# First block's attention in batches of three branches per pair of heads and tile of queries, with the local branch's rows scaled on POOL

## The reference, cut to what matters

```python
s = jnp.einsum('bgnqd,bgkd->bgnqk', qb, k_cmp) * scale - slopes * d_c
p_cmp = masked_softmax(s, d_c >= 0)
o_cmp = jnp.einsum('bgnqk,bgkd->bgnqd', p_cmp, v_cmp)
...   # o_slc and o_win in the same way, from two other sets of keys and values
return g[..., 0:1] * o_cmp + g[..., 1:2] * o_slc + g[..., 2:3] * o_win
...
return o * jax.nn.silu(z)      # z = h @ its columns of w_in
```

## Time and profile before

| | us |
|---|---|
| median of 3 runs | 3018.0 |
| the profiled execution | 3018.1 |
| its span, first to last instruction | 3016.3 |
| attention stage, PE's first scores to its last product | 194.0 to 422.5 |

### The profile page before, as it was taken

How to read it: one execution, slowest core, us unless ns; L and a number is a source line. 1 busy time by engine, 2 the same in 40 slices (tenths; PEclk the granted TensorE clock), 3 DMA queues, 4 the chain that set the end, 5 groups by cost and what they waited for, 6 DMA issues and landing times. The chain is left out here.

```text
span 3016.3 us, 40331 instructions
## 1 busy us (share of the span) xinstructions
PE 2877.6 (95%) x16205; PEld 2346.1 (78%) x16205; DVE 1359.6 (45%) x2458; ACT 1139.6 (38%) x2067; POOL 1237.9 (41%) x593
## 2 busy tenths in 40 slices
PE   6999989999999979999998999999998999999998
PEld 4875558888988867677887999988787757888887
DVE  5436650342133233683542555532477642566620
ACT  4347762222244333343553422222343355422221
POOL 5432224454344432222222545554445422545553
PEclk9999999999999988999997999999999999999999
DMA  7310012222322211113222422233222223422222
GB/s 263 140 57 15 15 32 94 98 98 98 112 91 98 97 43 55 42 43 100 75 75 90 150 84 95 90 103 105 87 92 80 86 74 103 160 91 97 98 99 91
DMA packets 83457, 272.70 MB, mean 90 GB/s; under 512 B 9863, under 2 KB 10119, under 8 KB 83144
## 3 DMA queue, kind: packets, MB, share of 16 engines
q1 hardware_dynamic: 81936, 269.23, 26.8%
q10 hardware_dynamic: 1336, 0.89, 0.1%
HBM read 255.34 MB, written 14.75 MB: 90 GB/s over the span
## 5 line engine op out<-in xcount | busy, mean ns | idle before, releaser
L132 POOL TENSOR_TENSOR weights_lo<-weights_raw,weights_hi 128x1024 fp32r<-128x1024 f32 x415 | 1008.3, 2432 | 1356.6 <-ACT weights_hi L124 1356.4
L124 ACT ACTIVATE weights_hi<-weights_raw 128x1024 fp32r<-128x1024 f32 x415 | 437.6, 1058 | 1049.7 <-PE acc L491 540.8
L489 PE MATMUL acc<-h_hi,weights_hi 128*128 128x512 f32 (+2 forms) x1808 | 667.1, 369 | 28.3 <-ACT gate_tiles L2554 7.9
L490 PE MATMUL acc<-h_lo,weights_hi 128*128 128x512 f32 (+2 forms) x1808 | 640.1, 354 | 0.0
L491 PE MATMUL acc<-h_hi,weights_lo 128*128 128x512 f32 (+2 forms) x1808 | 639.7, 354 | 0.0
L489 PEld LDWEIGHTS acc<-h_hi,weights_hi 128*128 128x128 f32 x1808 | 346.4, 192 | 108.7 <-issue 53.0
L491 PEld LDWEIGHTS acc<-h_hi,weights_lo 128*128 128x128 f32 x1808 | 346.7, 192 | 45.9
L490 PEld LDWEIGHTS acc<-h_lo,weights_hi 128*128 128x128 f32 x1808 | 347.4, 192 | 41.5 <-issue 0.2
L535 PE MATMUL acc<-weights_hi,h_hi 128*128 128x256 f32 (+1 forms) x480 | 145.3, 303 | 8.0 <-DVE h_lo L997 5.2
L489 PE MATMUL acc<-y_hi,weights_hi 128*128 128x512 f32 (+2 forms) x392 | 141.6, 361 | 10.1 <-DVE full L2744 5.2
L825 ACT ACTIVATE probs<-probs,low 128x31 f32<-128x31 f32 (+5 forms) x276 | 138.4, 503 | 19.8 <-DVE low L792 19.2
(11 more groups left out here) (435 smaller groups left out, 5247.4 us busy)
## 6 DMA issues: line engine op xcount, KB each, us to landing
weights_raw<-in_stream SPq DMA_DIRECT2D x415, 512.0 KB, 3.4
weight_ring<-in_w_ada SPq DMA_DIRECT2D x24, 512.5 KB, 7.5
gates<-gate_tiles SPq DMA_DIRECT2D x24, 258.0 KB, 4.2
gate<-gates SPq DMA_DIRECT2D x8, 774.0 KB, 5.7
held<-gates SPq DMA_DIRECT2D x8, 768.0 KB, 6.0
gates<-gate_tiles SPq DMA_DIRECT2D x23, 256.0 KB, 4.1
flipped<-bias_rows SPq DMA_DIRECT2D x8, 320.0 KB, 4.3
x<-in_x SPq DMA_DIRECT2D x2, 1024.0 KB, 13.6
```

Source lines behind the costliest of these rows:

```text
L124: act.activation(self.hi[:, at % CUT, :], self.raw[:, at % RAW, :], ACT.Copy).then_inc(self.hi_done, 1)
L132: pool.tensor_tensor(self.lo[:, at % CUT, :], self.raw[:, at % RAW, :], self.hi[:, at % CUT, :].bitcast(F32), ALU.subtract).then_inc(self. ...
L489: pe.matmul(out, left[0], right[0], start=start, stop=False)
L490: pe.matmul(out, left[0], right[1], start=False, stop=False)
```

## The change

`BatchAttend` replaces `PairAttend` in this stage alone (the second and third blocks keep it). A batch is all three kinds for one pair and one tile: 32 batches.

- Step s on PE: weigh(s-3) for all kinds, scores(s) for all kinds, then the turns of batch s-2, four parts (selected and window for each head) in units of at most 512 columns: 1 unit for tile 0, 2 for tile 1, 4 for tiles 2 and 3. There is one `turn` bank and one set of four score banks. A slot is one unit, so a step has 1, 2 or 4 slots, 92 in all.
- On ACT a step is copy out, then for each unit a read and up to two (of 4 units), three (of 2) or six (of 1) exponentials of batch s.
- On DVE a step is six minima of batch s, one reciprocal for all six sums of batch s-1, the scaling of the selected and compressed rows (four), and a copy of the turned compressed rows of batch s-2 from PSUM (`cmp_t`), which PE's next weigh waits for.
- The window's rows (the local branch) are scaled on POOL, behind its tables.
- The compressed kind of both heads is one matmul (block-diagonal `k_blk`, `v_blk`, cleared by POOL in the stage before, filled by two copies each) and one turn of 128x128.
- `Dense` has one `acc` bank here, taken at the unit's last slot. The lead is 8 slots instead of 16, here and in `gated_output`.

```diff
+class BatchAttend(Lane):
+    SETS, TURN, WEIGH = 3, 2, 3
+    PARTS, STATS = 4, 6
...
+        self.scores = psum("scores", [P, self.PARTS, 512])
+        self.turn = psum("turn", [P, 512])
+        self.out = psum("out", [P, 512])
+        self.small = psum("small", [P, 512])
...
+    def units(self, b):
+        per = max(1, 512 // self.keys_of(b))
+        return [range(a, min(a + per, self.PARTS)) for a in range(0, self.PARTS, per)]
...
+    def pool(self, pool):
+        pool.memset(self.probs_cmp[:, :, :], 0.0).then_inc(self.cleared, 1)
+        for s, subs in enumerate(self.subs):
+            n = (s - 1) // self.T + 1
+            if s >= 1 and (s - 1) % self.T == 0 and n < NH // 2:
...
+                self.build(pool, n).then_inc(self.built, 1)
+            if 1 <= s <= self.N:
+                pool.wait_ge(self.row_inverted, s)
+                for stat in (2, 3):
+                    self.share(pool, s - 1, stat).then_inc(self.window_ready, 1)
...
+        for s, subs in enumerate(self.subs):
+            b = s - self.TURN
+            if 0 <= s - self.WEIGH < self.N:
+                weigh(s - self.WEIGH)
+            if s < self.N:
+                scores(s)
+            for u in range(subs):
+                if 0 <= b < self.N:
+                    turn(b, u)
+                    if u == subs - 1:
+                        turn_cmp(b)
+                yield
...
+            if s < self.N:
+                for stat in range(self.STATS):
+                    lowest(s, stat)
+            if 1 <= s <= self.N:
+                invert(s - 1)
+                for stat in (0, 1, 4, 5):
+                    self.share(dve, s - 1, stat).then_inc(self.weights_ready, 1)
+            if 0 <= s - self.TURN < self.N:
+                read_cmp(s - self.TURN)
...
-            dense = Dense(sem, psum, ws, [unit for i in range(KT) for unit in feature_units(ws, i, h, 1, S, act=keep(i))], KT)
-            attention = PairAttend(sem, sbuf_of, psum, k, groups, False, S, tables=(build_tables, [per * n for n in range(NH // 2)]), score_sets=2)
-            run.lanes(paced((dense.weights, ahead(dense, 2 * KT), 1), (attention.weights, 0, 1)), [dense, attention], 2 * KT)
+            dense = Dense(sem, psum, ws, [unit for i in range(KT) for unit in feature_units(ws, i, h, 1, S, act=keep(i))], KT, banks=1)
+            attention = BatchAttend(sem, sbuf_of, psum, k, q, y, k_blk, v_blk, keys, v_tok, gates, table, table_cmp, build_tables)
+            run.lanes(paced((dense.weights, ahead(dense, KT), 1), (attention.weights, 0, 1)), [dense, attention], KT)
...
-            run.lanes(order, [dense, cut], 2 * KT)
+            run.lanes(order, [dense, cut], KT)
```

More of the change, by code:

```diff
@@ L1 @@
+import itertools
 import math
@@ L462, in act @@
                         self.ws.round(act, self.first, c + AHEAD)
-                if k == min(3, unit.ks - 1) and u >= 1:
+                if self.banks > 1 and k == min(3, unit.ks - 1) and u >= 1:
                     finish(u - 1)
+                if self.banks == 1 and k == unit.ks - 1:
+                    finish(u)
                 yield
-        finish(len(self.units) - 1)
+        if self.banks > 1:
+            finish(len(self.units) - 1)
         for c in self.late:
@@ L1599, in dve, with pool @@
         dve.wait_ge(self.out_ready, 1)
-        dve.tensor_copy(self.k_cmp[:, :], self.out[:, 0, 0:NKV * N_CMP]).then_inc(self.copied, 1)
+        dve.wait_ge(self.cleared, 2)
+        by_group = self.out[:, 0, 0:NKV * N_CMP].rearrange("p (g n) -> p g n", g=NKV)
+        for m in range(2):
+            rows = slice(m * HD, (m + 1) * HD)
+            dve.tensor_copy(self.k_blk[rows, :, 32 * m:32 * m + N_CMP], by_group[rows]).then_inc(self.copied, 1)
         yield
         dve.wait_ge(self.out_ready, 2)
-        dve.tensor_copy(self.v_cmp[0:N_CMP, :], self.out[0:N_CMP, 1, 0:NKV * HD]).then_inc(self.copied, 1)
+        by_group = self.out[0:N_CMP, 1, 0:NKV * HD].rearrange("p (g d) -> p g d", g=NKV)
+        for m in range(2):
+            dve.tensor_copy(self.v_blk[32 * m:32 * m + N_CMP, :, m * HD:(m + 1) * HD], by_group).then_inc(self.copied, 1)
+        yield
+    def pool(self, pool):
+        pool.memset(self.k_blk[:, :, :], 0.0).then_inc(self.cleared, 1)
+        pool.memset(self.v_blk[:, :, :], 0.0).then_inc(self.cleared, 1)
         yield
@@ L1796, in sparse_mixer @@
             dense = Dense(sem, psum, ws, units, NKV + 6)
-            compressed = Compress(sem, sbuf_of, psum, k, A, kv, k_cmp, v_cmp)
+            compressed = Compress(sem, sbuf_of, psum, k, A, kv, k_blk, v_blk)
             distances = Distances(sem, k, A, distance, distance_cmp, gates, build_tables, lambda dve: dense.wait_unit(dve, NKV + 2 * (S // P)))
```

163 lines of the change are left out of this document (159 added, 4 removed).

## The result

| | before | after |
|---|---|---|
| median, us | 3018.1 (4 runs, 3017.8 to 3018.8) | 3039.4 (4 runs, 3035.2 to 3041.8) |
| ratio to before, 95% interval | | 1.0064, 1.0052 to 1.0077 |
| span of the profiled execution | 3016.3 | 3033.5 |
| PE's first scores to its last product with values | 194.0 to 422.5 | 187.6 to 446.8 |
| TensorE clock at half in that stage | none | 4 falls, 23.9 us |

The change costs 21.3 us, and the forecast was 3038 with 3008 to 3068.

What follows compares the result with a forecast made beforehand. PE was taken as the attention stage's limit before, a cross-engine chain after. Rounds of 30.7 + 0.6 + 0.9 + 0.2 = 32.4 us put its end 25.8 later: 3018.1 + 25.8 - 5 = 3038.9, about 3038, range 3008 to 3068.

Steps and rivals of the forecast that it cites:

- the chain: Attention steps: PE's run-up, then ACT's alternating reads and exponentials, neither covering the other; 30.7 us per round before the dense lane.
- the removed work: PE in the attention stage: fewer score matmuls, turns and products, 0.5 us per batch, 16 us plus 1 for tile 0.
- the extras: Charges added to each attention round for dense slots, ACT's part of the dense lane and POOL's hold-up of DVE: 0.6, 0.9, 0.2.
- 0.6 for dense slots: PE in the attention stage: dense slots fall into holes behind turns, charged 0.1 us each, 0.6 in a round.
- 0.9 for ACT's part of the lane: ACT in the attention stage: z reads and roundings, 1.4 us per unit, two thirds in the chain, 0.9 in a round.
- 0.2 for POOL: DVE held up by POOL's scaling, felt only in the step where DVE is last: 0.2 us in a round (0 to 1).
- rival 3: PE's clock falls to half in the drain and now and then in the stage, 10 to 20 us: 3053, chance 0.12.
- Start, steps, drain: Attention stage: starts at 188.5, first three steps end about 198.2, then more steps and a 15.8 us drain, ending at 448.3.
- The next stage: Behind attention: the shorter lead costs nothing, ACT's first silu comes sooner and PE waits less; 5 us given back.
- Rival 2: POOL's scaling holds DVE for its whole length, 3.4 us in a round on the path: 3062, chance 0.13.
- the table's row: Earlier profile row of POOL's table, 2.02 us on POOL with 0.5 lost on DVE, read as disagreeing with whole-instruction exclusion.
- Rival 1: PE stays the attention stage's limit, a round being PE's own 26.5 us less part of the waits: 2996, chance 0.12.

Runs made afterwards that it cites:

- e2: The changed kernel with each step's scores put ahead of the products with values on PE: 3008.7 us, ratio 0.9963.
- e4: The changed kernel with one of three products kept in each slot of the attention stage's dense lane: 3064.9 us, ratio 1.0148.
- e3: The kernel before the change, with a lead of 8 dense slots instead of 16 in `gated_output` alone: 3015.1 us, ratio 0.9981.
- e1: The changed kernel with the window's rows scaled on DVE again instead of POOL: 3047.3 us, ratio 1.0088.
- e10: e2 with ACT's first two exponentials of a step ahead of its first read and its copy out: 3005.8 us, ratio 0.9955.

## Why the prediction was right

The sign and the mechanism were right: PE's holes behind the chain, not the removed work, set the stage. That the number is within 2 us is luck, since the errors of its terms cancelled: the chain and part of the extras too high, the clock left out.

- **The chain.** 30.7 was reckoned for a bare round, and 30.7 is the measured one with the lane in it, where the clock holds. Single steps, from weigh to weigh, were 7.3, 9.1, 7.0 and 7.3 in the sum for tiles 0 to 3, and 7.35, 8.94, 7.44 and 7.21 on the mean in the trace (tile 3 without its falls). The shortest of each kind are 6.93, 8.53, 7.31 and 7.21, 30.0 in a round, which is the better measure of the bare chain: the sum was 0.7 too high, with the steps of tiles 0 and 1 too long and that of tile 2, which DVE ends, too short. e2 tests the chain best: take it apart, and 30 us go.
- **The extras, 1.7 in a round: mis-sized.** 0.6 for dense slots, 0.9 for ACT's part of the lane and 0.2 for POOL came to 13 us. The slots' 0.6 doesn't show: e4's clean steps without two thirds of the slots' work are the same, so the holes take them. The lane's 0.9 does show. The steps that score tile 0 took 8.42 to 9.31 (turn to turn) in the four in which ACT has a read of z or a rounding, and 7.88 to 8.22 in the other three, and over all four kinds the clean mean is 1.0 in a round above the shortest steps. POOL subtracts behind most of these roundings, and the two are not separated here.
- **The clock: zero in the forecast.** It was rival 3, and it came along with the forecast instead of in its place: about 10 us in the steps. It fell in the stage, not in the drain. Three of four falls begin within 0.9 us of one place, where PE waits for DVE behind the minima of tile 2 (0.94) and for the copy `cmp_t` (1.50):

```profile
322.44 0.30 PE L984 MATMUL small<-const,probs_cmp 128*128 128x128 f32 x1 [0.94 <-DVE low L1050]
324.24 0.80 PE L1007 MATMUL out<-cmp_t,v_blk 128*128 128x128 f32 x2 [1.50 <-DVE cmp_t L1063]
...
326.01 3.79 PE L967 MATMUL scores<-keys_t,q 64*128 64x512 f32 x8
```

  The half clock then meets the step with most work in one piece: scores of 512 keys take 3.79 instead of 1.99.
- **Start, steps, drain.** Step 3 starts at 199.7 (198.2 said), steps 3 to 31 take 231.3 (234.3), the drain 15.8 (15.8). The last product is at 446.8 against 448.3.
- **The next stage** gave back less than 5: the last product is 24.3 later than before and the end of the third unit 21.6, that of the fourth 21.1, so about 3. Its first split product, as the earlier trace rows:

```profile
461.62 0.47 PE L496 MATMUL acc<-y_hi,weights_hi 128*128 128x512 f32 x1 [3.43 <-POOL weights_lo L133]
```

  It comes 14.8 behind the stage and came 13.9 behind it, so PE waits 0.9 more here. From it to the end of the third unit it takes 6.7 now and took 10.3: the later waits are shorter, and the 3.4 us at half clock that before had there (the 0.59 of the earlier trace rows) are gone in after. In before the lead alone is worth 4.7 (e3). In the two profiled executions the difference is 20.9 at the scores that begin at 1453.9 in before and 17.2 at those that begin at 2478.0; what gives these 3.7 back is not known.
- **POOL.** 512 columns were said to take 1.5 and take 0.99, the other sizes 0.81, 0.64 and 0.48. DVE's row beside it is 0.74 on the mean, half of them at 0.55 and half at 0.93. Rival 2, which had DVE held for all of each POOL instruction, would have shown rows of 1.5 or more; held against their lengths in before, DVE's scalings lose 14.6 us beside POOL's, 1.8 in a round, where rival 2 had 3.4 on the path. The prediction took the table's row as evidence against the rule of the Trainium skill (SBUF — State Buffer, section "SBUF: two separate sides"). The trace of after agrees with the rule in that the engine that comes second waits for the end of the other's instruction (the 52 of 53 above). It does not agree for the whole of a long instruction: a DVE scaling of 31 columns took its usual 0.29, from 0.97 us into one of POOL's 1.83 us tables (128x640), and only the next one was held until the table's end. e1 gives the value of the move, 7 us.
- **Rival 1** was not wrong as a limit, only not reached by this order: e2 and e10 come to a round of 27, where it said 26.5, and PE is busy for 87% of e2's stage. The removed work was also more than the 17 us of the sum: PE is busy 196.3 in e2's stage, and before it was 215.3 with 8 slots (5.6) less.

## What to carry to other kernels

When batching removes work from the busiest engine, write out the new step as a chain over all engines before counting the gain: here 24 us of work went and the stage's last product came 24 us later, and putting the next step's scores ahead of this step's products (no instruction added or removed) turned +21 into -11. With the exponentials ahead of the copy out it was -14, a step that the intervals don't tell from none. Work that depends on nothing late belongs ahead of a wait, on each engine's own list. Where PE is no longer the limit, count its clock as well, and look at what stands behind each hole.

## What the runs showed of the hardware

- Less work on PE made the program slower by 25 us (e4): with PE busy for 79% of the stage the granted clock was 0.95 on the mean, and with two thirds of the dense work gone 0.85. A further us at half cost 0.38 us in this stage, which a chain sets; for PE's own work alone, done at half speed, the estimate is 0.5.
- DVE and POOL take turns on SBUF (after): each DVE scaling that is held ends a fixed time behind the end of POOL's instruction, 0.28 us for 512 columns and 0.03 for 31. POOL's scaling of 512 in turn takes 1.04 where DVE's stands ahead of it and 0.93 otherwise.
- A TENSOR_SCALAR with two factors is not dearer on POOL than the tables' with one: 1.9 ns per column (0.99 us for 512), against 2.9 (1.87 for 640). Why the tables' is the dearer one was not tested.
- An idle f32 product of 128x128 costs PE 0.24 (2.17 / 9), a turn of the same size 0.15 (0.59 / 4, the prediction's price); the products are recorded as two instructions each, the turns as one.
